# Where three token tiles of the MLP input are turned, and when they are split, in a two-layer hybrid decoder trunk

## The reference, cut to what matters

```python
def hybrid_layer(x, ...):
    h = rms_norm(x, ln_mix_pre)
    ...                                  # three token mixers, gated: merged (512, 1024)
    x = x + rms_norm(merged @ w_out, ln_mix_post)
    h2 = rms_norm(x, ln_mlp_pre)
    ff = jnp.square(jax.nn.relu(h2 @ w_up)) @ w_down
    return x + rms_norm(ff, ln_mlp_post)
```

## Time and profile before

| quantity | value |
|---|---|
| runs, median (lowest to highest) | 2002.19 us (2001.02 to 2003.47) |
| the profiled execution, its own time | 2001.97 us |
| its span | 2000.2 us |
| mean granted TensorE clock | 0.987 of full |
| PEld (weight loads) busy | 1552.1 us, 78% |
| DVE (VectorE) busy | 1067.6 us, 53% |
| ACT (ScalarE) busy | 474.2 us, 24% |
| POOL (GpSimd) busy | 1024.3 us, 51% |
| HBM traffic | 93 GB/s over the span |

### The profile page before, as it was taken

How to read it: one execution, slowest core, us unless ns; L and a number is a source line. 1 busy time by engine, 2 the same in 40 slices (tenths; PEclk the granted TensorE clock), 3 DMA queues, 4 the chain that set the end, 5 groups by cost and what they waited for, 6 DMA issues and landing times.

```text
span 2000.2 us, 25269 instructions
## 1 busy us (share of the span) xinstructions
PE 1928.5 (96%) x8926; PEld 1552.1 (78%) x8926; DVE 1067.6 (53%) x1686; ACT 474.2 (24%) x923; POOL 1024.3 (51%) x821
## 2 busy tenths in 40 slices
PE   8999999999999999999999999999999999999998
PEld 7876667788778888888878667677887788888887
DVE  5754798743464550363366547987435646403623
ACT  3153243221323100011222533523113241000111
POOL 5663443335670666666346534342456607666662
PEclk9999999999999999999999999999999999999999
DMA  6332112222520322222222311122125204222321
GB/s 241 133 122 68 56 61 71 80 74 74 200 95 1 138 95 95 95 98 92 84 85 95 127 58 64 63 72 79 64 74 210 84 1 147 94 95 97 102 93 57
DMA packets 72475, 186.77 MB, mean 93 GB/s; under 512 B 18304, under 2 KB 30784, under 8 KB 71488
## 3 DMA queue, kind: packets, MB, share of 16 engines
q1 hardware_dynamic: 41328, 152.10, 22.2%
q10 hardware_dynamic: 31056, 33.38, 5.0%
HBM read 174.40 MB, written 11.06 MB: 93 GB/s over the span
## 4 chain that ended last, share of the span: by engine, by line
PE 77%; DVE 15%; ACT 4%; issue 3%; POOL 1%; DMA 0%; DVEq 0%; SPq 0%; POOLq 0%; ACTq 0%
PE psD L1008 19%; PE psD L1009 19%; PE psD L1010 19%; PE psM L1008 3%; PE psM L1009 3%; PE psM L1010 3%; DVE work L2047 3%; DVE small L2045 3%; PE psM L1067 2%; PE psM L1074 2%; PE psM L1164 1%; PE psM L1172 1%; DVE x L1946 1%; POOL w_lo L982 1%; ACT wide L1508 1%
## 5 line engine op out<-in xcount | busy, mean ns | idle before, releaser
L982 POOL TENSOR_TENSOR w_lo<-raw,w_hi 128x1024 fp32r<-128x1024 f32 x272 | 672.8, 2473 | 22.7
L1008 PE MATMUL psD<-a_hi,w_hi 128*128 128x512 f32 (+2 forms) x1488 | 601.3, 404 | 10.0 <-DVE a_lo L2170 6.6
L1010 PE MATMUL psD<-a_hi,w_lo 128*128 128x512 f32 (+2 forms) x1488 | 578.4, 389 | 0.0
L1009 PE MATMUL psD<-a_lo,w_hi 128*128 128x512 f32 (+2 forms) x1488 | 578.3, 389 | 0.0
L977 POOL TENSOR_TENSOR w_hi<-raw,tabs 128x1 fp32r<-128x1 f32 x272 | 62.7, 230 | 916.9 <-PE psD L1010 806.7
L1008 PEld LDWEIGHTS psD<-a_hi,w_hi 128*128 128x128 f32 (+1 forms) x1488 | 281.9, 189 | 89.8 <-issue 30.2
L1009 PEld LDWEIGHTS psD<-a_lo,w_hi 128*128 128x128 f32 (+1 forms) x1488 | 281.9, 189 | 59.7 <-issue 5.7
L1010 PEld LDWEIGHTS psD<-a_hi,w_lo 128*128 128x128 f32 (+1 forms) x1488 | 281.5, 189 | 58.8 <-issue 0.4
L978 POOL TENSOR_SCALAR w_hi<-raw 128x1023 fp32r<-128x1023 f32 x272 | 297.8, 1095 | 0.0
L2200 DVE TENSOR_TENSOR f_lo<-gt,f_hi 128x512 f32 x64 | 127.4, 1990 | 59.3 <-ACT f_hi L1766 59.3
L1766 ACT CAST f_hi<-gt 128x512 f32 x64 | 39.8, 622 | 479.7 <-DVE gt L2197 479.7
(11 more groups left out here) (268 smaller groups left out, 2720.7 us busy)
## 6 DMA issues: line engine op xcount, KB each, us to landing
raw<-in_ws SPq DMA_DIRECT2D x272, 512.0 KB, 3.2
s_raw<-in_wo ACTq DMA_DIRECT2D x14, 512.0 KB, 11.4
out<-x SPq DMA_DIRECT2D x8, 512.0 KB, 5.5
x<-rows_d ACTq DMA_DIRECT2D x4, 1024.0 KB, 6.8
x<-out ACTq DMA_DIRECT2D x2, 2048.0 KB, 8.2
e_raw<-in_wo ACTq DMA_DIRECT2D x8, 512.0 KB, 6.5
tabs<-in_tab SPq DMA_DIRECT2D x1, 2944.0 KB, 11.4
x<-in_x SPq DMA_DIRECT2D x4, 512.0 KB, 5.3
```

What stands on the lines that cost most here:

```text
L982: pool.tensor_tensor(w_lo[:, s, :], raw[:, s, :], w_hi[:, s, :].bitcast(F32), ALU.subtract) \
L1008: pe.matmul(out, lhi, rhi, start=start, stop=False)
L1009: pe.matmul(out, lhi, rlo, start=False, stop=False)
L1010: return pe.matmul(out, llo, rhi, start=False, stop=stop)
```

## The change

On TensorE the turn of tile 0 moves into out tile 2, ahead of its slab j = 2. The turn of tile 1 moves into the same out tile, ahead of slab j = 5. The turn of tile 2 moves into out tile 3, ahead of slab j = 5. On ScalarE and VectorE the splits of tiles 0 and 1 now stand behind the second norm of tile 1, and the split of tile 2 behind the second norm of tile 2. The turn and the split of tile 3 stay last. No instruction is added or taken away, the waits of each turn and split stay as written, and the banks stay the same.

```diff
--- before.py
+++ after.py
@@ -63,6 +63,7 @@
 HPITCH = BLOCKS * BPITCH
 STAYING = [("out", k, 2, half * S, S) for half, k in ((0, 2), (0, 4), (0, 6), (1, 0), (1, 2), (1, 4), (1, 6))]
 READY = ST - 1
+TURNS = {(2, 2): 0, (2, 5): 1, (3, 5): 2}
 PIECES = 4
 
 
@@ -1339,6 +1340,8 @@
 
                     def out_tile(t):
                         for j, (_, k, ks, c, _) in enumerate(STAYING):
+                            if (t, j) in TURNS:
+                                turn_x1(TURNS[t, j])
                             if t == 0:
                                 pe.wait_ge(*on("s_lo", j + 1))
                                 pe.wait_ge(*on("a_lo", KT + k + 2))
@@ -1358,12 +1361,8 @@
                                 ins = pe.matmul(x1_T(t, k), x[:, t, cut(k)], wide[:, t, 0:P], start=True, stop=True)
                             ins.then_inc(*inc("x1_turned", 1))
 
-                    for t in range(READY):
+                    for t in range(ST):
                         out_tile(t)
-                    for t in range(READY - 1):
-                        turn_x1(t)
-                    out_tile(ST - 1)
-                    turn_x1(READY - 1)
 
                     def up_tokens(i, t0, t1):
                         for k in range(KT):
@@ -1739,14 +1738,11 @@
                             act.wait_ge(*on("out_tile", 2 * t + half + 1))
                             squares("post_mix", t, half, (psM, psD)[half][t][:, :])
                         root("post_mix", t, 2)
-                        if t == READY:
-                            hi_x1(READY - 1)
                         act.wait_ge(*on("x1", t + 1))
                         squares("pre_mlp", t, 0, x[:, t, :])
                         root("pre_mlp", t, 1)
-                        if t == READY - 1:
-                            for i in range(READY - 1):
-                                hi_x1(i)
+                        for i in {1: (0, 1), 2: (2,)}.get(t, ()):
+                            hi_x1(i)
                     hi_x1(READY)
 
                     act.wait_ge(*on("a_lo", 2 * KT + ST * KT))
@@ -2179,12 +2175,9 @@
                         own("gained")
                         sig(dve.scalar_tensor_tensor(out=x[:, t, :], in0=wide[:, t, :], scalar=r,
                                                      in1=x[:, t, :], op0=ALU.mult, op1=ALU.add), "x1")
-                        if t == READY:
-                            lo_x1(READY - 1)
                         diagonal("pre_mlp", t)
-                        if t == READY - 1:
-                            for i in range(READY - 1):
-                                lo_x1(i)
+                        for i in {1: (0, 1), 2: (2,)}.get(t, ()):
+                            lo_x1(i)
                     lo_x1(READY)
 
                     def hidden(g):
```

## The result

| | before | after |
|---|---|---|
| runs, median (lowest to highest) | 2002.83 us (2001.02 to 2007.04, 6 runs) | 1994.0 us (1993.08 to 1995.17, 6 runs) |
| ratio | 1 | 0.9948, interval 0.9933 to 0.9963 |
| profiled execution, its span | 2001.97, 2000.2 us | 1994.1, 1992.3 us |

The change makes the kernel faster, by 0.52%. Three further runs of before had 2006.1, 2001.1 and 2007.04 us: the first three were the low part of a wide spread. Over the batches of the experiments the median of before was 2003.4 to 2004.8 us. By the medians of one batch the gain is 8.8 to 11.0 us, where 6.3 were forecast.

The account below looks back on a forecast made before the run. TensorE, busy for 96% of the span, was taken as the bound, with time won at its stops. Savings of 3.81 us (first layer) and 2.45 us (second), 6.26 in all, took 2001.97 to 1995.7 us; range 1993.2 to 1998.5.

Parts of the forecast that it names:

- The stop, its cause and its end: TensorE's 2.57 us wait before the up projection, each layer: tile 2's split queued behind tile 3's first norm; would be gone.
- The turns: Turns of tiles 0 to 2 inside out tiles, 1.85 us each with the return; 0.1 us of wait allowed at tile 2's.
- ScalarE and VectorE in time: Both engines finish the early splits before tile 2's norm needs them, by 0.6 and 0.4 us.
- Rival A: The wait comes back at the turn of tile 2, its diagonal late by 1.3 us a layer: 1998.3 us; chance 0.12.
- The turn of tile 3 next in line, with 1.7 us in hand: Next to be late after out tile 3: its diagonal at 643.6, TensorE there at 645.3; slack down from over 7 us.
- Rival C: Turns among large matmuls drop the clock within the out tiles; kernel slower, about 2004.5 us; chance 0.05.
- The clock term: First layer's up projection after the stop runs at full clock, saving 1.36 us once; the later slow stretch stays.
- Rival B: The later slow stretch of the first layer, worth 1.55 us, goes too: 1994.2 us; chance 0.13.
- The weighing of the free-running watch: Clock watch does not restart with the kernel, so 1.36 and 1.55 us are draws per execution: gain 4.9 to 7.8 us.

Follow-up runs that it names:

- e5: Kernel before with TensorE's order unchanged; only the split of tile 2 moved, behind tile 2's own norm on ScalarE and VectorE: 2000.59 us, ratio 0.9983.
- e12: Changed kernel with seven 512-column matmuls, result unread, behind out tile 0, so the rest of the stage comes later: 2002.25 us, ratio 0.9990 against before.
- e3: Kernel before with only the turns and splits of tiles 0 and 1 moved, tile 2's left in place: 2004.36 us, ratio 0.9993.
- e11: Kernel before, unchanged, one more profiled execution to see the clock in the two stages: 2003.81 us.
- e13: Changed kernel with fifteen 512-column matmuls, result unread, behind out tile 0: 2002.17 us, ratio 0.9991 against before.
- e9: Kernel before with all three stops of the stage (2.57, 0.73 and 1.20 us) filled with matmuls whose result nobody reads: 2002.83 us, ratio 0.9993.
- e1: The changed kernel once more, unaltered, beside other runs on one chip: 1993.61 us, ratio 0.9944 against before.
- e4: Kernel before with eleven 512-column matmuls, result unread, laid into the 2.57 us stop: 2002.48 us, ratio 0.9988.
- e8: Changed kernel with a TensorE wait ahead of the up projection that puts the stop back: 1999.80 us, ratio 0.9985 against before.

## Why the prediction was too small

*The stop, its cause and its end: right.* The 2.57 us were a place in three queues, and are gone in both layers. e5 divides them as the forecast's chain has it, the turn's own 0.8 us left when only the split moves.

*The turns: right.* Forecast 614.95, 620.88, 632.25 and 636.92 us; measured, less 1.35, 614.95, 620.83, 632.15 and 636.78. A turn between slabs costs 1.80 us (616.30 to 618.00 and 0.10 for the return) where I took 1.85, and there was no 0.1 us of wait. With the 48 matmuls at 8.35 for 8.40, that makes the full-clock gain 2.70 us a layer where 2.45 were forecast, 0.5 us in the sum.

*ScalarE and VectorE in time: right.* The gain products of tile 2 stood 1.1 us apart (626.52, 627.62), and VectorE waited 0.4 us before the second, the slack that was worked out. Rival A did not happen.

*The turn of tile 3 next in line, with 1.7 us in hand: right,* 1.6 measured. Rival C is out: the clock is 1.00 through the out tiles.

*The clock term: mis-sized, and this is the step that failed.* It stood at 1.36 us in the sum; the mean granted clock of all executions (0.9874 and 0.9904) makes it some 4 to 6 us, and what the gain has over the 5.4 us of work is 3.4 to 5.6. The sum counted 1.36 us of clock, the slow stretch behind the stop in the one layer that had it, and left the later one "where it is in the sum, since the stops before it stay". Both terms took a slow stretch to belong to the stop ahead of it. e12 and e5 show that the same 1.20 us stop brings one or not by when it comes, and the change moved it by 2.7 to 4.1 us. Between the two profiles 5.4 us are work and 1.3 + 2.6 clock, less the 1.35 us by which the later one came to the stage late. Rival B (0.13) named the later stretch and was right for this pair. What it lacked is the border of the layers, about 1 us, and that the second layer stands as near to its slow stretches as the first: in e3 they came in both layers at both places, though both profiles of before have none there. A second miss lies in the starting point. The profiled execution of before, at 2001.97 us, and the three runs beside it were 2 us below the kernel's usual 2004. That was luck: e11 had the same slow stretches in the stage, came to it 1.6 us later (592.26 against 590.67) and took 2003.81.

*The weighing of the free-running watch: half wrong.* The prediction took from the Trainium skill ("TensorE: Matmul & The Clock Gate", "What's actually happening") that the same code meets the watch at different points, and made the clock a draw of each execution, a gain of 4.9 to 7.8 us. Measured from the start of the program the slow stretches do differ between executions. But measured from the slow stretch near 370 us, the stage keeps its place to within 0.7 us in 33 of 34 cases. So at the 1.20 us stop the clock is mostly a fixed number of the kernel, which a change can move. At the 2.57 us stop of the kernel before it did remain a draw, since a few hundredths of a microsecond decide there; the changed kernel has taken that draw away.

*What stays open.* That the moment decides is shown for the stage by e12, e13 and the table. The delay in both was made of matmuls at full rate; one of the same length without matmuls was not run. Why the stage keeps its distance from the stretch near 370 us no run here shows. Open are also why filling the stops (e9) brings back less time than clock, and what is left of e13's 1.5 to 2.4 us.

## What to carry to other kernels

When an operation is late because of its place in a queue, list for each engine what stands in front of it and when its data were ready; the timeline gives the new finish of such a move to about 0.1 us. A slow-clock stretch in one profile is not a term that stays or goes with the stop ahead of it: compare the two layers, or two executions, and keep room for it on both sides. After a move, test with a dummy delay of a microsecond or two whether the gain is the work or its alignment: here 5.4 us were the work, and some 5 us of clock went when all came 1.6 us later. Compare the mean granted clock of all executions, too: in e1, e5 and e12 it told work from clock, where one profile could not.

## What was not expected of the hardware

A delay of 1.57 us in each of two stages cost 8.2 us (e12), while twice that delay left the clock of both stages at 1.00 (e13), though it cost as much in time. Where a slow stretch began in the middle of the 128-column matmuls it lasted 10 us (e4 and e8, first layer), 5.8 us of it in these matmuls, the rest in the 512-column ones behind them; those that began at the 1.20 us stop were a third as long. A stop of 2.57 us brought a slow stretch when it ended up to 270.22 us behind the one near 370 us, and none from 270.26 on. Going over from fp32r slabs to an fp32 turn and back costs 0.10 us, and waits that are already met ahead of a turn cost nothing that the timeline shows.
